# A state-space branch whose small products get operands stacked in two parts by way of memory

## The reference, cut to what matters

```python
u = xin.reshape(bsz, seq, 64, 16)
bb_re = k_re[..., None] * b_re - k_im[..., None] * b_im
bb_im = k_re[..., None] * b_im + k_im[..., None] * b_re
bu_re = einsum('blgh,gph->blgp', u, bb_re)
bu_im = einsum('blgh,gph->blgp', u, bb_im)
# a scan over positions: s = a * s + bu, complex
y = einsum('blgp,ghp->blgh', s_re, c_re) - einsum('blgp,ghp->blgh', s_im, c_im)
```

## Time and profile before

| | |
|---|---|
| median of 3 runs | 2958.08 us (2958.06 to 2958.66) |
| the profiled execution, its own time | 2958.22 us |
| its span in the profile | 2956.4 us |
| TensorE's granted clock, mean | 1.0 of full |
| TensorE busy | 2944.8 us |
| VectorE busy | 1978.1 us |
| ScalarE busy | 1731.1 us |
| DMA, mean over the span | 199 GB/s |

### The profile page before, as it was taken

How to read it: one execution, slowest core, us unless ns; L and a number is a source line. 1 busy time by engine, 2 the same in 40 slices (tenths; PEclk the granted TensorE clock), 3 DMA queues, 4 the chain that set the end, 5 groups by cost and what they waited for, 6 DMA issues and landing times.

```text
span 2956.4 us, 37411 instructions
## 1 busy us (share of the span) xinstructions
PE 2944.8 (100%) x13302; PEld 2427.1 (82%) x13302; DVE 1978.1 (67%) x2104; ACT 1731.1 (59%) x2454; POOL 441.8 (15%) x423
## 2 busy tenths in 40 slices
PE   9999999999999999999999999999999999999998
PEld 7888888888888888888887788888888888888887
DVE  6777754566667777676778886655556666666666
ACT  6876644547655555555675576554557554555555
POOL 1000110110035243320235450111000000000000
PEclk9999999999999999999999999999999999999999
DMA  8656666756666676676765555766656666666664
GB/s 259 185 157 199 199 200 194 200 182 200 192 192 221 191 225 198 214 222 190 262 193 197 195 186 168 219 206 209 206 202 186 199 192 195 193 192 192 192 192 163
DMA packets 298844, 588.43 MB, mean 199 GB/s; under 512 B 18464, under 2 KB 18480, under 8 KB 298352
## 3 DMA queue, kind: packets, MB, share of 16 engines
q1 hardware_dynamic: 292352, 563.61, 61.7%
q0 software_dynamic: 5952, 22.77, 2.5%
q10 hardware_dynamic: 432, 0.62, 0.1%
HBM read 574.35 MB, written 12.58 MB: 199 GB/s over the span
## 4 chain that ended last, share of the span: by engine, by line
PE 94%; DVE 2%; ACT 2%; issue 1%; DMA 1%; DVEq 0%; SPq 0%; ACTq 0%
PE banks L1733 94%; DMA raw<-in_w_in 1%; ACT whi L616 1%; DVE wlo L1117 1%; PE banks L1736 0%; ACT W L616 0%; ACT L616 0%; DVE W L1530 0%; DVE W L1522 0%; DVE banks L1523 0%; DVE banks L1525 0%; ACT G L616 0%; DMA Z<-in_x_t 0%; DVE W L1545 0%; DVE WR L1547 0%
## 5 line engine op out<-in xcount | busy, mean ns | idle before, releaser
L1117 DVE TENSOR_TENSOR wlo<-raw,whi 128x1024 fp32r<-128x1024 f32 x1047 | 1353.3, 1298 | 869.4 <-ACT whi L616 862.5
L616 ACT ACTIVATE whi<-raw 128x1024 fp32r<-128x1024 f32 (+1 forms) x1049 | 1105.9, 1059 | 1037.1 <-PE banks L1733 966.0
L1733 PE MATMUL banks<-whi,Y 128*128 128x512 f32 x4800 | 1484.6, 389 | 0.3 <-DVE W L1216 0.2
L1733 PEld LDWEIGHTS banks<-whi,Y 128*128 128x128 f32 x4800 | 901.1, 188 | 188.2 <-issue 0.9
L1733 PE MATMUL banks<-wlo,Y 128*128 128x512 f32 x2400 | 933.7, 389 | 0.0
L1733 PE MATMUL banks<-whi,XH 128*128 128x512 f32 x1792 | 705.2, 394 | 2.3 <-DVE wlo L1117 1.9
L1733 PE MATMUL banks<-whi,XL 128*128 128x512 f32 x1792 | 698.1, 390 | 0.0
L1733 PE MATMUL banks<-wlo,XH 128*128 128x512 f32 x1792 | 697.6, 389 | 0.0
L1733 PEld LDWEIGHTS banks<-wlo,Y 128*128 128x128 f32 x2400 | 450.6, 188 | 93.0
L1733 PEld LDWEIGHTS banks<-whi,XH 128*128 128x128 f32 x1792 | 336.5, 188 | 78.9 <-issue 7.9
L1733 PEld LDWEIGHTS banks<-whi,XL 128*128 128x128 f32 x1792 | 336.3, 188 | 71.2
(11 more groups left out here) (254 smaller groups left out, 1184.1 us busy)
## 6 DMA issues: line engine op xcount, KB each, us to landing
raw<-in_w_in SPq DMA_DIRECT2D x383, 512.0 KB, 3.9
raw<-in_w_mlp_up SPq DMA_DIRECT2D x128, 512.0 KB, 4.0
raw<-in_w_mlp_down SPq DMA_DIRECT2D x128, 512.0 KB, 3.9
raw<-in_w_mlp_in SPq DMA_DIRECT2D x128, 512.0 KB, 3.8
raw<-in_w_mlp_out SPq DMA_DIRECT2D x128, 512.0 KB, 3.7
raw<-in_w_branch SPq DMA_DIRECT2D x80, 512.0 KB, 4.2
raw<-in_w_out SPq DMA_DIRECT2D x64, 512.0 KB, 4.4
tables<-G POOLq DMA_DIRECT2D x8, 1024.0 KB, 8.2
```

The lines of the kernel that those rows point to most:

```text
L616: return nc.scalar.activation(out_, in_, f, **kw)
L1117: tt(wlo[:, i % RING, :], raw[:, i % RING, :], whi[:, i % RING, :].bitcast(F32), ALU.subtract)\
L1733: return nc.tensor.matmul(out_, l, r, start=start, stop=stop, **kw)
```

## The change

B and the inputs are each split into a high and a low part, and the parts are stacked so that one fp32r matmul over all 128 partitions gives the sum of all four products: the partitions of the B operand hold 32 rows of the high part, the same 32 again, then 32 of the low part, and the same again; those of the input operand hold 32 high, 32 low, 32 high, 32 low. The stacks are put together by way of memory:

- B is fetched by GpSimd in one transfer in a new layout, split by ScalarE (two copies at positions 4 and 5) and VectorE (two subtractions at 6 and 7), and stored to `s5_b` by SP in four pieces at positions 12, 16, 20 and 24.
- The inputs are split in two halves (ScalarE at positions 21 and 29, VectorE at 22 and 31) and stored to `s5_u` from ScalarE's queue, four transfers each at positions 22, 23, 33 and 35.
- For each m, SP's `load_stack` issues three fetches: B's high part and B's low part, each a source of [2, 32, 512] with step 0 in the dimension of 2, into 64 partitions; and the inputs, a source of [2, 64, 512] likewise, into 128 partitions. Stack 0 stands at position 30, stack 1 at 33, stack m from 2 on at 26 + 5m + 1. Two stack buffers alternate.
- `s5_in` waits for its stack and issues four matmuls of 128 rows x 128 columns by 256 columns. The one of m = 0 stands after unit 28 instead of 26; the others stay where they were.
- Several semaphores are merged under common names, with the counts changed to fit.

```diff
+            def s5_parts():
+                for n in range(4):
+                    yield 12 + 4 * n
+                    if n == 0:
+                        sp_.wait_ge(S("s5_lo"), 2)
+                    h, part = n // 2, n % 2
+                    sp_.dma_start(A["s5_b"][8 * h:8 * h + 8, part].rearrange("m (c x) n -> m c x n", x=4),
+                                  (BHI, BLO)[part][64 * h:64 * h + 64].bitcast(F32)).then_inc(S("s5_saved"), 16)
+                yield 30
+                sp_.wait_ge(S("s5_saved"), SAVED[1])
+                load_stack(0)
+                yield 33
+                load_stack(1)
+                for m in range(2, 16):
+                    yield S5Q + S5D * m + 1
+                    if m == 8:
+                        sp_.wait_ge(S("s5_saved"), SAVED[2])
+                    sp_.wait_ge(S("bu_mm"), 2 * m - 2)
+                    load_stack(m)
+
+            def load_stack(m):
+                for part in range(2):
+                    sp_.dma_start(slot(Y, 3)[64 * part:64 * part + 64, CH * (m % 2):CH * (m % 2) + CH].bitcast(F32),
+                                  A["s5_b"][m, part].unsqueeze(0).to_broadcast([2, 32, CH])).then_inc(S(f"s5_stack_in{m % 2}"), 16)
+                sp_.dma_start(slot(Y, 2)[:, CH * (m % 2):CH * (m % 2) + CH].bitcast(F32),
+                              A["s5_u"][m // 2, m % 2].rearrange("k c e t -> (k c) (e t)").unsqueeze(0).to_broadcast([2, 64, CH]))\
+                    .then_inc(S(f"s5_stack_in{m % 2}"), 16)
...
+            def save_inputs(h, part):
+                act.wait_ge(S(("s5_hi", "s5_lo")[part]), 3 + h)
+                m = (UHI, ULO)[part][h]
+                for c in range(4):
+                    act.dma_start(A["s5_u"][4 * h:4 * h + 4, c // 2, part, :, c % 2, :].rearrange("i c t -> c i t"),
+                                  m[32 * c:32 * c + 32].bitcast(F32).rearrange("p (i t) -> p i t", t=T))\
+                        .then_inc(S("s5_saved"), 16)
...
             def s5a():
 
+                for r in range(2):
+                    yield 4 + r
+                    act.wait_ge(S("s5_b_in"), 16)
+                    a(BHI[:, SL * r:SL * r + SL], BRAW[:, SL * r:SL * r + SL]).then_inc(S("s5_hi"), 1)
+                yield 21
+                act.wait_ge(S("stage_turned2"), 1)
+                a(UHI[0], UIN[0]).then_inc(S("s5_hi"), 1)
+                yield 22
+                save_inputs(0, 0)
+                yield 23
+                save_inputs(0, 1)
+                yield 29
+                act.wait_ge(S("stage_turned2"), 2)
+                act.wait_ge(S("c_scaled"), 1)
+                a(UHI[1], UIN[1]).then_inc(S("s5_hi"), 1)
+                act.wait_ge(S("s5_saved"), SAVED[1])
+                yield 33
+                save_inputs(1, 0)
+                yield 35
+                save_inputs(1, 1)
...
             def s5_in():
                 for m in range(16):
-                    yield S5Q + S5D * m
-                    i, c0 = m // 2, 64 * (m % 2)
-                    if m == 0:
-                        pe.wait_ge(S("s5_b_in"), 32)
-                        pe.wait_ge(S("stage_turned2"), 1)
-                    else:
-                        if m == 8:
-                            pe.wait_ge(S("stage_turned2"), 2)
+                    yield S5Q + S5D * m + (0 if m else 2)
+                    pe.wait_ge(S(f"s5_stack_in{m % 2}"), 48 * (m // 2 + 1))
+                    if m:
                         pe.wait_ge(S("s5_r_ready"), 2 * m)
                     for r in range(2):
                         for e in range(2):
-                            c = c0 + 32 * e
-                            ins = mm(PU[e][:, T * r:T * r + T], BT[r][c:c + 32, i, :], XI[c:c + 32, i, :],
-                                     tile_position=(c, 0))
+                            ins = mm(PU[e][:, T * r:T * r + T], SB[m % 2][:, r, e, :], SU[m % 2][:, e, :])
                     ins.then_inc(S("bu_mm"), 2)
```

More of the change, by code:

```diff
@@ L247, in build @@
         GMG = slot(W, 11)
-        BT = [slot(Z, 2 + r).rearrange("p (i c) -> p i c", i=8) for r in range(2)]
+        BRAW, BHI, BLO = slot(Z, 2, 2), slot(WR, 6, 2), slot(WR, 8, 2)
+        UIN, UHI, ULO = ([slot(t, i) for i in at] for t, at in ((W, (2, 3)), (WR, (4, 13)), (WR, (5, 5))))
+        SU = [slot(Y, 2)[:, CH * i:CH * i + CH].rearrange("p (e t) -> p e t", e=2) for i in range(2)]
+        SB = [slot(Y, 3)[:, CH * i:CH * i + CH].rearrange("p (r e s) -> p r e s", r=2, e=2) for i in range(2)]
         CT = [slot(Z, 8 + r).rearrange("p (i c) -> p i c", i=8) for r in range(2)]
@@ L270, in build @@
         GLUQ = [8, 9, 11, 12]
+        SAVED = [64, 192, 320]
         def s5_place(j):
@@ L383, in tables @@
                     if j == 0:
-                        sp_.wait_ge(S("tables_saved"), 32 * S5_TILES // TG)
+                        sp_.wait_ge(S("scratch_saved"), 32 * S5_TILES // TG)
                     if j >= NTAB:
@@ L401, in _ @@
                 branch = Steps(tables() if b == 2 else iter(()))
+                stacks = Steps(s5_parts() if b == 2 else iter(()))
                 for ph in "ab":
@@ L413, in _ @@
                             branch.upto(ch.u0 + i - u0[b, "a"])
+                            stacks.upto(ch.u0 + i - u0[b, "a"])
                 up = rows("w_mlp_up" if b == 1 else "w_mlp_in_2")
@@ L486, in block2 @@
                 pool.wait_ge(used, mlp_base(1, NF - 1))
+                pool.dma_start(BRAW, A["b_t"]).then_inc(S("s5_b_in"), 16)
                 for r in range(2):
[L488 to L491, removed]
+                    pool.dma_start(CT[r], A["c_t"][r]).then_inc(S("small2_in"), 16)
+                pool.dma_start(GW, A["gm_w_t"]).then_inc(S("small2_in"), 16)
                 pool.wait_ge(evict["dve"], down0[1] + NF * NCH)
-                pool.dma_start(A["x1"].rearrange("(t p) n -> p t n", p=P), X).then_inc(S("x_saved"), 16)
-                pool.wait_ge(S("gm_w_in"), 16)
+                pool.dma_start(A["x1"].rearrange("(t p) n -> p t n", p=P), X).then_inc(S("scratch_saved"), 16)
+                pool.wait_ge(S("small2_in"), 48)
                 nc.gpsimd.affine_select(out=GW, in_=GW, compare_op=ALU.is_ge, fill=0.0, base=0,
@@ L503, in block2 @@
                 kr, ki, nkr = (k.unsqueeze(2).to_broadcast([P, 32, 32]) for k in (D_KR, D_KI, D_NKR))
-                pool.wait_ge(S("s5_c_in"), 32)
                 pool.wait_ge(S("s5_factors"), 1)
@@ L529, in block2 @@
                         if j == 24:
-                            pool.dma_start(GMG, A["gm_norm_g_2"][0].partition_broadcast(P)).then_inc(S("gm_gain_in"), 16)
+                            pool.dma_start(GMG, A["gm_norm_g_2"][0].partition_broadcast(P)).then_inc(S("gain_in"), 16)
                         else:
@@ L543, in make_tables @@
                     if g:
-                        pool.wait_ge(S("tables_saved"), 32 * g)
+                        pool.wait_ge(S("scratch_saved"), 32 * g)
                     nc.gpsimd.memset(c[:, :, 0:1], 1.0)
@@ L562, in make_tables @@
                         pool.dma_start(A["tables"][TG * g:TG * g + TG, :, i, :].rearrange("j p t -> p j t"), m)\
-                            .then_inc(S("tables_saved"), 16)
-                pool.wait_ge(S("tables_saved"), 32 * S5_TILES // TG)
+                            .then_inc(S("scratch_saved"), 16)
+                pool.wait_ge(S("scratch_saved"), 32 * S5_TILES // TG)
             def load_bias(n, k):
@@ L584, in _ @@
                     load_biases(3, 5)
-                    pool.wait_ge(S("x_saved"), 16)
+                    pool.wait_ge(S("scratch_saved"), 32 * S5_TILES // TG + 16)
                 for n in range(NCH):
@@ L771, in evictions @@
                         if b != blocks[0] and stages == 0:
-                            act.wait_ge(S("x_saved"), 16)
+                            act.wait_ge(S("scratch_saved"), 32 * S5_TILES // TG + 16)
                         if stages >= 2:
@@ L921, in s5a @@
                     act.wait_ge(S("s5_g"), 1)
-                    a(YH[:, 8 + 4 * h:12 + 4 * h, :], GS[:, 4 * h:4 * h + 4, :]).then_inc(S("s5_g_hi"), 1)
+                    a(YH[:, 8 + 4 * h:12 + 4 * h, :], GS[:, 4 * h:4 * h + 4, :]).then_inc(S("s5_hi"), 1)
             def attn2():
@@ L1560, in gmlp @@
                 chain(nc.vector.reciprocal(grs, grs))
-                dve.wait_ge(S("gm_gain_in"), 16)
+                dve.wait_ge(S("gain_in"), 16)
                 for t in range(NT):
@@ L1577, in gmlp, with s5_lo @@
                     y_lo(2, 0, 2 * n, 2, PU[n % 2].rearrange("p (k t) -> p k t", t=T), n + 1)
-            def s5_g_lo():
+            def s5_lo():
+                for r in range(2):
+                    yield 6 + r
+                    dve.wait_ge(S("s5_hi"), 1 + r)
+                    c = slice(SL * r, SL * r + SL)
+                    tt(BLO[:, c], BRAW[:, c], BHI[:, c].bitcast(F32), ALU.subtract).then_inc(S("s5_lo"), 1)
+                for h in range(2):
+                    yield (22, 31)[h]
```

(19 more changed lines are left out.)

## The result

The changed kernel takes 3025.2 us (median of 4 runs, 3023.56 to 3030.07) against 2958.07 us: a ratio of 1.0229, 95% interval 1.0212 to 1.0247, so 67 us slower. The forecast was 3023 us. The profiled execution has a span of 3023.1 us, 66.7 more than before.

What follows compares the result with a forecast made beforehand. It took TensorE's own instruction stream as the bound. To 2958.22 us it added 64.5 us of lateness from two DMA engines, TensorE's 10.5 us saving not counted: 3022.7, so 3023 us; whole range 2949 to 3055.

Steps and rivals of the forecast that it cites:

- The chain: In the state-space stretch, a late `raw` delays ScalarE's copy, then VectorE's subtraction, then TensorE; 20.6 us per period against about 15.
- "over 10": Profile sign: weight loads behind the stack fetches take over 10 us from issue to landing instead of 3.9.
- Two engines: Stack fetches with outermost dimension 2 put 128 packets on each of two DMA engines, none on 14; chance 0.70.
- The price of a packet: 92.0 ns per 2 KB packet on each of the two engines, 315.7 us for 3432 packets, stack 0 to unit 103's load.
- the 251.2 us available: Time from stack 0's issue to unit 103's start on TensorE, 255.9 us, less landing, copy and subtraction.
- two engines would have kept up: Rival: two engines carry the stacks without lateness, below 73 ns per packet; 2952 to 2958 us, chance 0.06.
- The sum: Whole kernel: 2958.22 us of the profiled execution plus 64.5 us lateness at unit 103 gives 3022.7, so 3023 us.
- The groups: Each `s5_in` group on TensorE falls from 1.26 to 0.54 us, saving 0.72; 10.5 us over 16 groups after deductions.
- the 0.15 that the forecast took off: After seven of 16 groups plain float32 `s5_out` follows at once, so the switch is still paid: 7 x 0.15 = 1 us.
- Group 0 two units later: VectorE's tiles 0 and 1 delay subtractions 30 and 31; TensorE waits 2.0 and 1.9 us, 3.9 us once.
- The rival of the other side: Stack packets spread over 16 engines and their fetches are hidden: 2951.6 us, between 2947 and 2959; chance 0.21.
- What was hidden: Added copies, subtractions, issues and stores before and around the branch stay off TensorE's path; 1 to 3 us if cover were gone.

## Why the prediction was right

*The chain.* As forecast: late `raw`, late copy, late subtraction, and TensorE waiting for it, 18 times in 16 periods. The weights' median of 8.9 us to landing is less than the "over 10" that was named as a sign, and the profile gives no time to landing for the stacks. Beside it TensorE waits 18.9 us for the stacks, which the forecast had left out of the price. Moving the fetches to ScalarE's queue traded one wait for the other at nearly the same time, as it would if both are the lateness of the same engines.

*Two engines.* The runs show that the source's outermost dimension makes the loss: 2, 4 and 32 give three times for the same bytes, and neither the step of 0, nor the bytes, nor the queue, nor the small groups do. That it does so by confining the packets to that many engines is inferred. The Trainium skill (DMA: Bandwidth & Descriptors, "Why a DMA increments its semaphore by 16 and not by 1") says that a transfer uses as many engines as the largest number up to 16 that divides the slowest dimension of both sides, here 2, 4 and 16; the three times, 3025.2, 2964.2 and 2955.8 us, fall in that order.
The forecast also assumed, without saying so, that all fetches take the same two engines. The price of a packet is what speaks for it.

*The price of a packet.* Forecast 92.0 ns from the densest stretch. The 64.9 us at unit 103 with the 251.2 us available make 316.1 us for 3432 packets, 92.1 ns, but this is a mean of unlike parts. The inputs' fetches of stacks 3, 12 and 15 are issued at 1556.69 (above), 1733.79 and 1797.68:

```profile
1733.79 0.54 SPq L418 DMA_DIRECT2D Y<-s_u  x1
...
1797.68 0.57 SPq L418 DMA_DIRECT2D Y<-s_u  x1
```

Nine periods of 224 packets in 177.1 us are 87.9 ns a packet; the last three, in 63.9 us, are 95.1 ns, and the 600 packets from stack 0 to stack 3 in 56.1 us are 93.5 ns. So the price of a packet was at most 88 ns where the pace was steadiest, 4% under the forecast, and at the start and in the attention stretch something else takes time as well.
The Trainium skill (DMA: Bandwidth & Descriptors, "Specifications") gives about 27 GiB/s per engine, an estimate of 71 ns a packet, with which two engines would have kept up; the measured pace decides against it here.

*The sum.* 64.5 us at unit 103 forecast, 64.9 measured; 3023 us forecast, 3025.2 measured. That agreement is in part luck. With 87.9 ns the forecast's own sum gives 301.7 us of work and 50.5 us of lateness; the missing 14 us are 8 in the first three and last three periods, 2 at the start, and 5 between the last stack and unit 103, for which it has no terms. The two errors cancel. The same kind of sum over the whole stretch was 14 us too low for the kernel with B alone over two engines, and a sum by period didn't find the loss there either.

*The groups.* Forecast 0.54 us a group. In the kernel with the other order of rows, where no transfer disturbs it, the four records begin 0.47 us ahead of the next unit:

```profile
1512.12 0.64 PE L1805 MATMUL banks<-Y 128*128 128x256 f32 x4
1512.59 0.40 PE L1805 MATMUL banks<-whi,XH 128*128 128x512 f32 x1
1512.83 0.40 PE L1805 MATMUL banks<-wlo,XH 128*128 128x512 f32 x1
```

That is 0.12 for each matmul, and the distance after them is 0.24 instead of 0.23. The group costs 0.48 us, so the saving is 0.78 against the forecast's 0.72. Where `s5_out` follows at once, group and `s5_out` together save 0.60 (from 1551.31 to 1553.69 before, from 1553.78 to 1555.56 now), 0.18 less; the 0.15 that the forecast took off for this stood on no row and was about right.

*Group 0 two units later.* Forecast 2.0 us of waiting at unit 30 and 1.9 at unit 31. The first was right, the second was right in size and wrong in kind:

```profile
1517.50 0.50 PE L1805 MATMUL banks<-whi,XH 128*128 128x512 f32 x1 [2.00 <-DVE wlo L1180]
...
1518.40 0.63 PE L1805 MATMUL banks<-whi,XH 128*128 128x512 f32 x1
1518.82 0.63 PE L1805 MATMUL banks<-wlo,XH 128*128 128x512 f32 x1
...
1521.38 0.50 PE L1805 MATMUL banks<-wlo,XH 128*128 128x512 f32 x1
1521.72 0.40 PE L1805 MATMUL banks<-whi,XL 128*128 128x512 f32 x1
1522.07 0.50 PE L1805 MATMUL banks<-whi,XH 128*128 128x512 f32 x1
```

After 2.0 us of idle time and three matmuls at full pace, they stand 0.43 us apart instead of 0.23, the clock's lower level. Unit 30 takes 4.57 us instead of 2.72, and by then unit 31's subtraction is done. The slow clock used up the second wait.

*The rival of the other side.* Spread over 16 engines, it said 2951.6 us; those kernels take 2955.6 to 2955.8. The step that failed in its sum is that nothing but TensorE's stream sets the end. It was true before the change and no longer after it. At group 9 the kernel with the other order of rows is 1.1 us ahead of the kernel before (1642.88 against 1643.97), where the sum has about 2; at the end it is 2.5 us ahead, where the sum has 6.6. Most of the difference is lost in the attention stretch, where the doubled groups cost almost nothing.

*What was hidden.* The added copies, subtractions, stores and issues of ScalarE didn't show: from 1407 to 1511 TensorE is busy for 103.93 of 104 us in the kernel before, in the changed one and in the one with the other order of rows. Group 0 begins at 1512.12 in the last, where the forecast had 1512.33.

The best version of the runs is the one with rows in the other order and tiles 0 and 1 later, 2954.1 us: 0.14% under the kernel before, below the 0.2% that I called measurable, though its interval excludes 1.

## What to carry to other kernels

Look at the outermost dimension of a DMA's source (the destination's was not varied here): with 2 there, 16 fetches of 512 KB cost 67 us, and the mean DMA share shows nothing of it (0.60 before and after). Put the repeated dimension inside, or make plain copies; both cost nothing here. A sum of work against time over a whole stretch can come out right by errors that cancel: check it against parts of the stretch. After shortening the engine that sets the pace, ask at once which engine is next.

## What was unexpected of the hardware

One wait of 2.0 us of TensorE was followed by 3 us of matmuls 0.43 us apart (granted clock 0.62 of full in 1517.5 to 1522), so a short stall cost nearly as much again, 1.85 us. It isn't so after every wait: in the kernel with the second subtraction at position 33, after the wait of 2.08 us, the granted clock is 1.00 in 1534.4 to 1539. And the 384 packets more on two engines that were at their limit already cost 109 ns each, above the mean of 92; whether the added ones cost more, or each of the 3816 a little (93.8 ns in the mean), the times don't tell.
